# Hybrid decoder step on eight cores: the final norm's result written to the feed-forward arena, and the next tile's input loaded directly behind it

## What is computed

```python
for layer in range(DEPTH):
    hp = rms_norm(xp, norm_mix[layer]);  hs = rms_norm(xs, norm_mix[layer])
    ...                                   # retention (layer 0) or windowed attention (layer 1)
    xp = xp + yp;  xs = xs + ys
    xp = xp + swiglu(rms_norm(xp, norm_ffn[layer]), ffn_w1[layer], ffn_w3[layer], ffn_w2[layer])
    xs = xs + swiglu(rms_norm(xs, norm_ffn[layer]), ffn_w1[layer], ffn_w3[layer], ffn_w2[layer])
y_prompt = rms_norm(xp, norm_final)
y_sample = rms_norm(xs, norm_final)
```

## Time and profile before

| | before |
|---|---|
| median of 3 runs (lowest to highest) | 2280.7 us (2278.78 to 2284.69) |
| the profiled execution, its own time | 2281.31 us |
| its span on the slowest core (core 7) | 2280.3 us |
| spans of the 8 cores | 2265.4 to 2280.3 us |
| mean granted TensorE clock, share of full | 0.953 to 0.961 |
| busy: PE, DVE (VectorE), ACT (ScalarE), POOL | 89%, 51%, 33%, 10% |
| DMA, mean over the span | 167 GB/s |

### The profile page before, as it was taken

One profiled execution on the slowest core, in us unless ns is written; L12 is line 12 of the kernel. 1 busy time (PEld: TensorE's weight loads), 2 busy tenths in 40 slices (PEclk: granted clock), 3 DMA queues, 4 the chain that ended last, 5 costly groups with the idle time before them and its releaser, 6 DMA issues.

```text
span 2280.3 us, 38746 instructions; the slowest of 8 cores (2265.4 to 2280.3 us)
## 1 busy us (share of the span) xinstructions
PE 2025.8 (89%) x12058; PEld 973.7 (43%) x12058; DVE 1170.4 (51%) x2770; ACT 758.7 (33%) x1480; POOL 225.4 (10%) x421
## 2 busy tenths in 40 slices
PE   5887998889988898969999878999899998998997
PEld 2433444334333344434444333434455554444554
DVE  3675455544456435446556456455445554555323
ACT  2323232332335224233333324333223442453111
POOL 1001011010122211101122012210000000000000
PEclk9998999999999999979999889999899999999998
DMA  8987797698766879645588676653433234231333
GB/s 193 210 190 146 216 210 200 163 236 192 213 207 197 224 197 187 112 148 177 163 227 226 195 216 206 201 196 126 151 103 100 102 117 114 91 99 64 115 131 107
DMA packets 128390, 380.27 MB, mean 167 GB/s; under 512 B 19744, under 2 KB 23968, under 8 KB 128160
## 3 DMA queue, kind: packets, MB, share of 16 engines
q1 hardware_dynamic: 81712, 240.15, 32.7%
q0 software_dynamic: 46480, 137.65, 28.9%
HBM read 341.43 MB, written 104.60 MB: 196 GB/s over the span
## 4 chain that ended last, share of the span: by engine, by line
PE 63%; DVE 16%; issue 8%; DMA 6%; ACT 5%; SPq 1%; DVEq 1%; POOL 0%; ACTq 0%; POOLq 0%
PE pb L529 61%; ACT arL L541 3%; DVE hT L554 2%; PE pb L535 2%; DVE arL L554 2%; DVE arL L563 2%; DMA arG<-st_in 2%; DVE stat L554 1%; DMA xT<-xTp 1%; DVE stat L816 1%; DVE arL L551 1%; DVE Sst L554 1%; DVE arG L554 1%; DMA wf<-wt 1%; DVE stat L557 1%
## 5 line engine op out<-in xcount | busy, mean ns | idle before, releaser
L529 PE MATMUL pb<-hT,wf 128*128 128x512 bf16 x2816 | 659.8, 384 | 21.6 <-DVE hT L554 4.2
L529 PEld LDWEIGHTS pb<-hT,wf 128*128 128x128 bf16 x2816 | 268.5, 99 | 348.7 <-issue 68.1
L529 PE MATMUL pb<-arF,wf 128*128 128x512 bf16 x1408 | 325.9, 383 | 5.9 <-ACT arL L541 2.3
L529 PE MATMUL pb<-wl,hT 128*128 128x512 bf16 (+1 forms) x1152 | 251.1, 370 | 3.6 <-ACT arG L541 2.6
L541 ACT ACTIVATE arL<-pb 128x512 bf16<-128x512 f32 (+2 forms) x262 | 189.0, 734 | 192.1 <-PE pb L529 157.0
L551 DVE TENSOR_TENSOR xT<-pb,xT 128x512 f32<-128x512 f32 x160 | 109.4, 689 | 213.8 <-PE pb L529 213.6
L554 DVE SCALAR_TENSOR_TENSOR arF<-arF,pb 128x512 f32<-128x512 f32 (+1 forms) x176 | 120.5, 686 | 179.6 <-ACT arF L541 121.9
L529 PEld LDWEIGHTS pb<-arF,wf 128*128 128x128 bf16 x1408 | 134.6, 98 | 162.0 <-issue 17.0
L541 ACT ACTIVATE arF<-pb 128x512 f32<-128x512 f32 (+1 forms) x192 | 114.7, 601 | 265.7 <-PE pb L529 260.1
L529 PE MATMUL pb<-arL,wl 128*128 128x512 bf16 (+1 forms) x832 | 198.6, 393 | 2.1 <-ACT arL L541 2.1
L529 PE MATMUL pb<-hT,wl 128*128 128x512 bf16 x800 | 194.3, 390 | 2.1 <-DVE hT L554 1.1
(11 more groups left out here) (98 smaller groups left out, 1978.5 us busy)
## 6 DMA issues: line engine op xcount, KB each, us to landing
wl<-wbd SPq DMA_DIRECT2D x123, 512.0 KB, 4.9
wf<-wbd SPq DMA_DIRECT2D x110, 512.0 KB, 4.3
arG<-st_in POOLq DMA_DIRECT2D x128, 256.0 KB, 5.4
srs<-arG POOLq DMA_DIRECT2D x128, 256.0 KB, 3.9
wf<-wbd SPq DMA_DIRECT2D x88, 352.0 KB, 3.5
wf<-wt POOLq DMA_DIRECT2D x50, 512.0 KB, 9.1
wl<-wt POOLq DMA_DIRECT2D x41, 512.0 KB, 11.3
wbd<-wl SPq DMA_DIRECT2D x41, 512.0 KB, 13.9
```

The source lines that it names most:

```text
L529: S.op("pe", lambda e: e.matmul(out, lhsT, rhs, start=start, stop=stop), r, w, d)
```

## The change

The final norm no longer scales in place. For each tile it resets the feed-forward arena `arF`, takes eight float32 pieces `y` of 512 columns there (8192 columns of bf16 width, for which the arena grows from 7680), and scales chunk by chunk from `xT` into them. The stores read `y`; they stay in SP's queue with the semaphore `yout`. Behind the store of chunk kc, `fin(0)` and `fin(1)` issue the load of chunk kc of tiles 2 and 3 in POOL's queue, and `swap` only norms.

```diff
-        LCOLS, FCOLS, GCOLS = 24832, 7680, 10880
+        LCOLS, FCOLS, GCOLS = 24832, 8192, 10880
...
-            def norm(cx, gi, P, to_x=False, after=None):
+            def norm(cx, gi, P, to_x=False, after=None, outs=None):
...
-                    stt(dst[:, kc, :NT], cx.xT[:, kc, :NT], gain(gi, kc), b2[:, :NT], ALU.mult, ALU.mult,
-                        [cx.xb[kc], bb2, spb], [db[kc]])
+                    dv, dvb = (dst[:, kc, :NT], db[kc]) if outs is None else outs(kc)
+                    stt(dv, cx.xT[:, kc, :NT], gain(gi, kc), b2[:, :NT], ALU.mult, ALU.mult,
+                        [cx.xb[kc], bb2, spb], [dvb])
                     if after is not None:
                         after(kc)
...
             def fin(t, P):
                 cx = pcx[t % 2]
+                ys = []
+
+                def outs(kc):
+                    if not ys:
+                        AF_.reset()
+                        for _ in range(KC):
+                            ys.append((AF_.alloc("y", [128, TT], F32), AF_.buf("y")))
+                    return ys[kc]
 
                 def after(kc):
-                    dma("sp", yout_p[kc][:, t * TT:(t + 1) * TT], cx.xT[:, kc, :], [cx.xb[kc]], [], "yout")
-                return norm(cx, 4, P, to_x=True, after=after)
+                    dma("sp", yout_p[kc][:, t * TT:(t + 1) * TT], ys[kc][0], [ys[kc][1]], [], "yout")
+                    if t < 2:
+                        load_xc(t + 2, kc)
+                return norm(cx, 4, P, to_x=True, after=after, outs=outs)
...
             def swap(t, P):
-                load_x(t)
-                yield
                 yield from norm(pcx[t % 2], 0, P)
```

More of the change, by code:

```diff
@@ L670, in load_x, with load_xc @@
             def load_x(t):
+                for kc in range(KC):
+                    load_xc(t, kc)
+            def load_xc(t, kc):
                 cx = pcx[t % 2]
-                for kc in range(KC):
-                    dma("sp" if t < 2 else "pool", cx.xT[:, kc, :], xin_p[kc][:, t * TT:(t + 1) * TT], [], [cx.xb[kc]], f"x{t}{kc}")
+                dma("sp" if t < 2 else "pool", cx.xT[:, kc, :], xin_p[kc][:, t * TT:(t + 1) * TT], [], [cx.xb[kc]], f"x{t}{kc}")
             def load_rope(t):
```

## The result

The changed kernel is slower: the ratio of its time to the time before is 1.0183, 95% interval 1.0155 to 1.021, which on 2281.9 us is +42 us (+35 to +48). Run again in another session it was 1.0174 (1.0128 to 1.022). Of its four executions two were disturbed on one die, so its plain median, 2339.14 us, says less than the ratio, which rests on the other two, 2315.87 and 2332.64 us. The profiled execution took 2315.87 us.

A forecast was written before the change was run, and what follows sets the result against it. PE's order was taken to bound the kernel, PE holding 63% of the chain that ended last. Terms -9 + 13 + 19 + 19 = +42 on the profiled 2281.3 us gave 2323 us, range 2306 to 2340.

The forecast's parts named there:

- main line: Whole kernel: scalings waiting for stores cost more than the early load gains; 2306 to 2340 us, chance 80%.
- Tile 2's load, -9: At fin(0), loads no longer wait for all eight stores: 9 us gained, bounds -12 to -4.
- 4.2 MB take 11.3 us: At fin(0), 16 stores and loads of 256 KB in flight together move at 371 GB/s, done by 1005.5.
- fin(1), +13: Tile 3's load: seven scalings wait for stores and PE stops behind VectorE; 7 x 3.3 - 10.1, bounds +5 to +18.
- L: Landing time of the store each next scaling waits for; taken as 3.3 us at fin(1), 2.2 at fin(2), 2.5 at fin(3).
- The page's price for L: Skill page's estimate, 2.6 us for 256 KB; would make the fin(1) term +8 and the sum some 3 us smaller.
- fin(2), +19: Seven waits delay the `arG` scalings PE needs: 0.8 + 15.4, plus 2.5 us of low clock; bounds +16 to +24.
- fin(3), +19: At the program's end, seven waits with nothing beside them add 7(L + 0.25) us; bounds +16 to +20.
- At nothing: Counted as free: scalings into `arF` stay 0.67 us, stage 5 and 6 activations' store waits, one exchange of PE rows.
- the chain costs nothing: Rival: store landings hidden or waits already met, tile 3's load gains 11 us too; 2261 us, chance 5%.
- only the end pays: Rival: other work covers PE at fin(1) and fin(2), only fin(3) loses 19 us; 2291 us, chance 4%.
- L is 5 at fin(1): Rival: landings as slow as before, 2.9 at fin(2), tile 2's load gains only 4; 2346 us, chance 9%.

The follow-up runs named there:

- chain_t1: As `own_sems`, but tile 0's and tile 1's stores share one semaphore, so scalings wait for the previous store at fin(1) alone; profiled 2288.0 us.
- own_sems: The changed kernel with one edit, a semaphore of their own for each tile's final-norm stores; ratio to the kernel before 0.9938, in another session 0.9947.
- chain_t2: As `own_sems`, but tile 2's stores share tile 0's semaphore, so scalings wait for the previous store at fin(2) alone; profiled 2296.8 us.
- chain_end: As `own_sems`, but tile 3's stores share tile 0's semaphore, so scalings wait for the previous store at fin(3) alone; profiled 2289.4 us.

## Why the prediction was right, point by point

2323 us was forecast, +42; the ratio gives +42, and the mechanism is that of the main line. The signs named for the profile came too: scalings 2.9 to 3.5 us apart, each released by `yTp<-arF`, PE stopped from 1310 for VectorE's additions, a stop of 15.35 us at fin(2). The terms were not all as well sized as their sum.

- **Tile 2's load, -9.** On core 7 PE reached the matmuls behind the sums 8.3 us sooner, and 8 was the figure in the working. But core 7 is the slowest core of before, and its stretch from fin(0), 315.7 us, was the longest of the eight (median 312.5), so there was more to gain there than elsewhere. Over the cores' medians the stretch gave 6.2 and 3.5 us in the change's two profiles, and 2.6 to 3.8 in the five others with the same instructions up to fin(1); six of these seven lie outside the bound of -4. The step that was too good is "4.2 MB take 11.3 us" at 371 GB/s. That rate was of stores alone; with stores, loads and weights in flight the busy engines moved anything from 197 to 388 GB/s.
- **fin(1), +13.** +7.8 and +8.0 by the change's two profiles. `chain_t1` gives +5.5 against before, which is the term's own measure, and +9.5 against `own_sems`, which already has the load's gain. The form held (32 matmuls, a stop of 16.30 us ended by the first addition, 0.4 us of PE's waits on squares); L was taken too large. The link was 3.35 us in the median over cores, 3.45 on core 7, so L is 2.4 to 2.5 and not 3.3 (in `chain_t1` a link of 3.08 on most cores, L 2.2), and 7 x 2.43 - 10.1 = +6.9. I chose 3.3 because the stores of this place landed after 3.8 us or more before. But there eight were in flight, here one store and at most a few loads: the nearest row by place was further off than the nearest by number in flight.
- **The page's price for L.** The Trainium skill, "DMA: Bandwidth & Descriptors", Anatomy of one DMA, gives a formula from which the estimate of 2.6 us for 256 KB comes. That section is about DMAs that GpSimd issues, which the prediction does not say; these stores stand in SP's queue, and landed after 2.0 us with nothing beside and about 2.4 at fin(1). For the fin(1) term 2.6 was nearer than my value; of the formula itself these stores are no test. The "some 3 us smaller" there does not come out either: 2.6 in all three terms gives 21 x 2.6 - 14 = +41, 1 us smaller, and in the fin(1) term alone 5 us. Which part of a landing is the receipt no run here shows.
- **fin(2), +19.** +17.9 and +17.5, `chain_t2` +19.0. The stop was 15.35 us; the low clock cost more than the 2.5 us counted: 2.93 for 16 matmuls that take 1.06 at full clock (2143.03) and 5.74 for 16 that take 3.62, 1.9 + 2.1 = 4.0 us (the first 16 took 1.44 before, so 0.4 of it stood there already). L was 2.03, not 2.2, 1.2 us less over seven links.
- **fin(3), +19.** +16.9 and +16.0, `chain_end` +16.3. L again: 2.03 for 2.5, seven times 0.47 = 3.3 us less. The row 2.4 to 2.6 was of eight stores in flight.
- **At nothing.** ScalarE's table load, its first instruction of stage 9, waited 31.8 us for the last store, until 2136.50. It held nothing up on core 7: PE had gone on at 2134.73, released by `arG`, and ran to 2148 without another stop.
- **The rivals.** That the chain costs nothing, that only the end pays and that L is 5 at fin(1) all fell; but cores 2 and 3 of `chain_t1`, with L = 3.3 and 3.55, show how near the last one can come on a single core.

The forecast terms sum to +42, the medians of the two profiles over the four stretches from fin(0) on to +36 and +38, and the slowest core's profiled span went up by 34.5. The errors partly cancelled: the load gained 3 to 6 us less than thought, the chain cost 8 to 10 less. That the forecast meets the ratio so closely is then in part luck.

The Trainium skill, "DMA: Bandwidth & Descriptors", section "Why a DMA increments its semaphore by 16 and not by 1", advises one semaphore for each slot in flight and not one for a stream, because a count shared by two DMAs can be passed too early. Here the shared count was the other danger: each wait took in every store issued so far. `own_sems`, with one for each tile, shows what that cost in this kernel: 1.0174 against 0.9938 side by side, and 1.0183 against 0.9947 in the two other sessions.

## What to carry to other kernels

Before a buffer is moved into an arena, look at what that arena's waits will be counted on: a DMA that never used it before becomes a wait of every later writer, and a semaphore shared by all stores makes that wait mean "the newest one". An own semaphore for each reuse cost nothing here and made the change a gain of 4 to 14 us, 0.2 to 0.6%, by how one counts; that version (`own_sems`) beats both kernels, and none of the others can be told to beat it.

Price a serial chain of DMAs by a landing with one in flight (2.0 us here with nothing beside, 2.2 to 2.4 beside loads), not by the landings of the burst that stood there before. Read a term from all cores and not from the slowest alone: that core is the one where the stop happened to be longest.

## What the runs showed of the hardware

A store of 256 KB from SP's queue with nothing beside it landed after 2.03 us nearly every time (minimum, median and maximum 2.0 us at fin(2)); eight in flight with eight loads of the same size took up to 15.5 us (`own_sems`, core 3). DMA engines busy at 98% or more moved anything from 197 to 388 GB/s. At fin(0) a stop behind the same instructions lasted 24.9 us where the neighbouring core did the same within 2.5 us, and 22.1 where it was over 5 us away; the reason was not tested. With the loads in SP's queue instead of GpSimd's they landed after 7.6 us in the median instead of 11.6 (core 3, fin(0)), and the time was the same.
